# Other SBUF addresses for the weight parts and the activation parts of a two-layer hybrid decoder on one core

## The reference, cut to what matters

```
h = rmsnorm(x); proj = h @ w_in                    # 1024 -> 10752 columns
A = dilated attention of 3 head groups; B = retention with decay, 4 heads
m = sigmoid(ga) * (A @ w_a) + sigmoid(gb) * (B @ w_b)
x = x + m @ w_o
x = x + relu(rmsnorm(x) @ w_up)**2 @ w_down        # 1024 -> 4096 -> 1024
```

## The kernel before

| tensor | before | after |
|---|---|---|
| h_hi, h_lo | 32, 32 | 32, 112 |
| w_hi slot 0, slot 1 | 32, 32 | 0, 16 |
| w_lo slot 0, slot 1 | 32, 32 | 32, 40 |
| z_hi, z_lo (also u) | 0, 0 | 96, 64 |
| m_hi, m_lo | 0, 0 | 0, 32 |
| y_hi, y_lo | 0, 0 | 64, 96 |
| x, w_raw | 32, 32 | 0, 0 |
| tables, rstd_all, decay, mask | 32 | 64 |
| the float32 tensors of attention and retention | 0 | 0 |
| ssum, sq, hn, relu, relu2, diag, gdiag (and others that share the end of the zone) | 0 | 0 |

## Time and profile before

### The profile page before, as it was taken

One profiled execution on the slowest core, in us unless ns is written; L12 is line 12 of the kernel. 1 busy time (PEld: TensorE's weight loads), 2 busy tenths in 40 slices (PEclk: granted clock), 3 DMA queues, 4 the chain that ended last, 5 costly groups with the idle time before them and its releaser, 6 DMA issues.

```text
span 1973.8 us, 26960 instructions
## 1 busy us (share of the span) xinstructions
PE 1957.8 (99%) x9580; PEld 1619.1 (82%) x9580; DVE 1110.7 (56%) x1764; ACT 730.5 (37%) x1124; POOL 91.5 (5%) x71
## 2 busy tenths in 40 slices
PE   8999999999999999999999999999999999999999
PEld 7987878887888888888899878888778888888887
DVE  5466675847446635444635574847655575445355
ACT  5134535354223323223322535453532233223233
POOL 0010110200000000000001110201000000000000
PEclk9999999999999999999999999999999999999999
DMA  4432322323232323232333322323233333323332
GB/s 135 128 91 65 101 83 65 102 65 96 93 98 89 105 85 106 85 106 85 106 110 86 91 81 76 91 65 102 61 101 96 97 95 97 101 90 97 94 96 76
DMA packets 208845, 182.20 MB, mean 92 GB/s; under 512 B 12624, under 2 KB 197072, under 8 KB 208496
## 3 DMA queue, kind: packets, MB, share of 16 engines
q1 hardware_dynamic: 208464, 180.65, 30.0%
q10 hardware_dynamic: 288, 0.28, 0.0%
HBM read 178.68 MB, written 2.23 MB: 92 GB/s over the span
## 4 chain that ended last, share of the span: by engine, by line
PE 95%; DVE 1%; ACT 1%; issue 1%; DMA 1%; SPq 0%; DVEq 0%; ACTq 0%
PE pj L1180 26%; PE pj L1182 25%; PE pj L1181 25%; PE rb L1327 2%; PE pj L1367 2%; PE sc L1270 2%; PE yo L1296 2%; PE pj L1368 2%; PE pj L1369 2%; PE pt L1280 1%; PE sc L1230 1%; PE sc L1232 1%; PE pt L1230 1%; PE pt L1232 1%; PE sc L1231 1%; PE pt L1231 1%
## 5 line engine op out<-in xcount | busy, mean ns | idle before, releaser
L1180 PE MATMUL pj<-h_hi,w_hi 128*128 128x512 f32 x1408 | 557.1, 396 | 0.0
L1182 PE MATMUL pj<-h_hi,w_lo 128*128 128x512 f32 x1408 | 548.5, 390 | 0.0
L1181 PE MATMUL pj<-h_lo,w_hi 128*128 128x512 f32 x1408 | 548.5, 390 | 0.0
L464 ACT CAST w_hi<-w_raw 128x1024 fp32r<-128x1024 f32 x330 | 331.7, 1048 | 395.8 <-PE pj L1182 263.5
L748 DVE TENSOR_TENSOR w_lo<-w_raw,w_hi 128x1024 fp32r<-128x1024 f32 x330 | 398.5, 1248 | 118.1 <-ACT w_hi L464 117.2
L1180 PEld LDWEIGHTS pj<-h_hi,w_hi 128*128 128x128 f32 x1408 | 264.2, 188 | 62.5 <-issue 6.9
L1181 PEld LDWEIGHTS pj<-h_lo,w_hi 128*128 128x128 f32 x1408 | 264.4, 188 | 56.0 <-issue 2.4
L1182 PEld LDWEIGHTS pj<-h_hi,w_lo 128*128 128x128 f32 x1408 | 264.3, 188 | 55.8
L1180 PE MATMUL pj<-z_hi,w_hi 128*128 128x512 f32 x640 | 253.2, 396 | 0.0
L1181 PE MATMUL pj<-z_lo,w_hi 128*128 128x512 f32 x640 | 253.2, 396 | 0.0
L1182 PE MATMUL pj<-z_hi,w_lo 128*128 128x512 f32 x640 | 253.2, 396 | 0.0
(11 more groups left out here) (169 smaller groups left out, 2301.8 us busy)
## 6 DMA issues: line engine op xcount, KB each, us to landing
w_raw<-in_w_in SPq DMA_DIRECT2D x152, 512.0 KB, 4.2
w_raw<-in_w_up SPq DMA_DIRECT2D x64, 512.0 KB, 4.0
w_raw<-in_w_down SPq DMA_DIRECT2D x64, 512.0 KB, 3.8
w_raw<-in_w_b SPq DMA_DIRECT2D x16, 512.0 KB, 4.1
w_raw<-in_w_o SPq DMA_DIRECT2D x16, 512.0 KB, 4.1
spread_share<-row_scratch SPq DMA_DIRECT2D x16, 256.0 KB, 3.9
w_raw<-in_w_a SPq DMA_DIRECT2D x8, 512.0 KB, 3.5
x_nat<-in_x SPq DMA_DIRECT2D x2, 1024.0 KB, 6.5
```

The lines of the kernel that those rows point to most:

```text
L464: nc.scalar.copy(w_hi[s][:, c], raw[:, c]).then_inc(hi_done, 1)
L1180: nc.tensor.matmul(out, w_hi[s][:, wc], acts[0], start=first, stop=False)
L1181: nc.tensor.matmul(out, w_hi[s][:, wc], acts[1], start=False, stop=False)
L1182: return nc.tensor.matmul(out, w_lo[s][:, wc], acts[0], start=False, stop=last)
```

## The change

Only addresses change. No instruction, wait or transfer is added, removed or moved: on each engine the program stands in the same order, with the same operations on the same shapes. Small fillers are put ahead of x, h_hi and h_lo, three tensors (h_lo and the second slots of w_hi and w_lo) get 8 more columns and are used from 16, 16 and 8 bytes behind their start, and the tensors of the zone that z, m and y share are placed one by one. The two names of the gate scratch, sA and sB, and the scratch that begins at `pad` move by a few hundred bytes with them.

```diff
-        fill = -nc.sbuf_base % 512
-        if fill:
-            sb("fill", [P, fill // 4], F32)
+        def phase(name, to):
+            base = -(-nc.sbuf_base // 32) * 32
+            fill = (to - base) % 128
+            if fill:
+                sb(name, [P, fill // 4], F32)
+        def shifted(name, n, skip):
+            return sb(name, [P, n + 8], F32R)[:, skip // 4:skip // 4 + n]
+        phase("fill_x", 0)
         x = sb("x", [P, KT, S], F32)
+        phase("fill_h_hi", 32)
         h_hi = sb("h_hi", [P, KT, S], F32R)
-        h_lo = sb("h_lo", [P, KT, S], F32R)
+        phase("fill_h_lo", 96)
+        h_lo = shifted("h_lo", KT * S, 16).rearrange("p (k s) -> p k s", k=KT)
         raw = sb("w_raw", [P, 2048], F32)
-        w_hi = [sb(f"w_hi{i}", [P, 2048], F32R) for i in range(2)]
-        w_lo = [sb(f"w_lo{i}", [P, 2048], F32R) for i in range(2)]
+        w_hi = [sb("w_hi0", [P, 2048], F32R), shifted("w_hi1", 2048, 16)]
+        w_lo = [sb("w_lo0", [P, 2048], F32R), shifted("w_lo1", 2048, 8)]
...
-        zone0 = -(-nc.sbuf_base // 512) * 512
+        zone0 = -(-nc.sbuf_base // 128) * 128
...
-        m_hi = at("G", "m_hi", [P, KT, S], F32R)
-        m_lo = at("G", "m_lo", [P, KT, S], F32R)
-        z_hi = at("G", "z_hi", [P, KT, S], F32R)
-        z_lo = at("G", "z_lo", [P, KT, S], F32R)
-        pad = top["G"]
-        y_hi = at("G", "y_hi", [P, KA, S], F32R)
-        y_lo = at("G", "y_lo", [P, KA, S], F32R)
+        def at_phase(name, k, to):
+            base = top.get("G", zone0)
+            top["G"] = base + (to - base % 128 + zone0 % 128) % 128
+            return at("G", name, [P, k, S], F32R)
+        m_hi = at_phase("m_hi", KT, 0)
+        m_lo = at_phase("m_lo", KT, 32)
+        z_hi = at_phase("z_hi", KT, 96)
+        z_lo = at_phase("z_lo", KT, 64)
+        pad = top["G"] + 64
+        y_hi = at_phase("y_hi", KA, 64)
+        y_lo = at_phase("y_lo", KA, 96)
+        top["G"] += 32
         sB = at("G", "sB", [P, 2, S], F32)
-        top["G"] += 5120
+        top["G"] = zone0 + 89 * 1024
         sA = at("G", "sA", [P, 2, S], F32)
```

## The result

| | before | changed |
|---|---|---|
| median us | 1977.8 (4 runs, 1976.58 to 1978.74) | 1996.62 (4 runs, 1996.01 to 1998.19) |
| the profiled execution | 1975.57 | 1996.29 |
| its span | 1973.8 | 1994.5 |

The ratio is 1.0097, 95% interval 1.0079 to 1.0114: the changed kernel is 1% slower, by 19 us where 11 were forecast. The lines of the code moved by 18 behind the edit (L1180 to L1182 are now L1198 to L1200).

The account below looks back on a forecast made before the run. PE, busy in 99% of the span, was taken to bound the kernel by its distances between matmul starts. Terms 15.8 - 5.5 + 0.8 = +11.1 us gave 1988 us; forecast 1978 to 1998, full range 1950 to 2008.

Parts of the forecast that it names:

- (a): 4224 matmuls with h moving: from 226.7 to 231.1 ns, 4.4 ns more on 3600 of them, +15.8 us.
- (d): Starts 16 or 8 bytes off in h_lo and the second weight slots: taken as 0, 6 us at most.
- single distances seen by weight slot: PE's trace after: the two weight slots may show different distances, unit by unit, proving that single distances matter; no size given.
- (b): 2496 matmuls with z, m and y moving: from 233.3 to 231.1 ns, -5.5 us; bounds -16.5 and +16.7 us.
- (c): Value products: 192 of 576 with 512 columns go from 226.7 to 231.1 ns, +0.8 us; 768 of 256 columns stay.
- (e): ACT and DVE casts and subtractions on the moved tensors: any lengthening hidden behind PE, waits near 11 us; transfers 0.
- z rhythm everywhere: Rival: any distance but 0 costs 233.3 ns, so h loses 23.8 us; 2001 us, 2007 with (d); chance 0.15, or worse included.
- A modest gain: Rival: distance 0 isn't the best, staggered pairs run faster; 1945 or 1961 us, if h's mean stays below 229 ns; chance 0.19.
- No change: Rival: z's slowness comes from its upper SBUF place or from addresses above 128 bytes, not the distance; 1977 us; chance 0.11.
- All interference gone: Rival: staggering removes all the excess per matmul, 127 us in all; 1850 us; chance 0.09.

Follow-up runs that it names:

- the first kernel on the pair that meets: Kernel before, with h_hi, w_hi, m_hi, z_lo, y_hi at 32 and h_lo, w_lo, m_lo, z_hi, y_lo at 96 modulo 128: 1997.38 us.
- The first experiment: Kernel before, with z, m and y moved to 32 modulo 128 like h and the weights: 1977.64 us, ratio 1.0003.
- the third and fourth scans: Kernel before, weights at 32 (slot 0) and 48 (slot 1) modulo 256; h at 32, then 208, with m, z, y moved too: 1977.16, then 1987.39 us.

## Why the prediction was right, and where it was off

**The direction and the mechanism held.** The forecast was 1988, slower; measured is 1996.6. No wait changed by more than 0.5 us, no engine but PE by more than 2 us, and h left its 226.7 ns. Against the +11.1 us of the sum the two spans differ by 20.7: h is 7.3 above its term, z, m and y 3.1, all else 0.7, and the values are 1.5 below theirs.

That 231.1 ns fits h so well is in part luck. I took it from nine matmuls that had distance 0 and came behind a float32 matmul; no row tied it to mixed distances. Of the mixtures measured later some ran at 231.1, but h's in the first kernel on the pair that meets ran at 232.2. And mixing isn't what costs: the uniform distances of 192 and 224 cost more, 233.3.

**(a), h, was sized 15.8 us and measured 23.1.** Three things are in the difference. The rate out of rhythm, 231.1 ns, was right for h's mixture at multiples of 32: 231.0 without the small shifts. The count was low: I left out 630 matmuls behind the restarts, but over all 4156 the mixture costs 17.1 us, 4.1 ns each. And the rest is (d).

**(d), the starts off 32 bytes, was the term that I mis-sized.** I bounded it by 6 us and took 0. The two kernels with and without the shifts differ by 6.0 us on h. Their profiled spans differ by 2.5 us (1994.5 against 1992.0), since z, m and y ran 0.9 us shorter with the shifts than without, the values 0.6, and the small matmuls and distances over 300 ns 2.0; their medians differ by 3.7 (1996.6 against 1992.9). The sign that the prediction named, single distances seen by weight slot, came only in part: in the changed kernel h's units of slot 0 run at 233.1, but those of slot 1 at 231.3 and at 233.3, so something besides the addresses counts here too. The two kernels also differ in the distances themselves by 8 and 16, so this is the cost of the shifts here, not a price of misalignment by itself. That 16 bytes off can cost much more is shown by the kernel with all at 48, 28 us above all at 32.

**(b), z, m and y, was sized -5.5 us and measured -2.4.** Out of rhythm z was to come to 231.1; it came to 232.4. With the same z addresses it did run at 231.1 against weights at 32 (-4.3 us), but at 233.3 against weights at 0 and 32. So mixtures of distances don't share one rate, as I took them to, but run at one of several between 231 and 233.3.

**(c), the values.** 512 columns +0.7 us where +0.8 was taken; 256 columns -1.4 us where 0 was.

**(e)** held: casts of 1047 ns and subtractions of 1250, waits unchanged.

**The reading of the distance was wrong in its modulus.** I took it modulo 128 as the change does, and the table of distances ahead of the prediction has a 0 for h that is 128 modulo 256. Modulo 256 its h distances are 160, 144 (w_hi with h_hi), 240, 224 (w_hi with h_lo) and 128, 120 (w_lo with h_hi). The forecast did not hang on it, since by either modulus h becomes a mixture. The first experiment did, and it missed.

**The rivals.** *z rhythm everywhere* gave 2001 and has come nearest to what happened: h at 232.7, z at 232.4. *A modest gain* fell with h's mean at 232.7 where its rule asked for less than 229. *No change* fell: the same instructions take 1961.7, 1977.6, 1990.0 and 2001.4 us by addresses alone. But one of its two reasons was half right: something in the addresses above 128 bytes does count, since z at 0 modulo 128 and 128 modulo 256 from the weights stayed at 233.3. The two independent read ports of which the Trainium skill's page "TensorE: Matmul & The Clock Gate" speaks (section "Step-by-step: what each phase is for") don't keep the operands' addresses from counting here. *All interference gone* did not happen in any of the kernels; no even stream of 512 columns was below 226.7.

## What to carry to other kernels

Where TensorE is busy throughout and streams moving operands of 4 bytes at the high clock, read the distance from start to start in each long stretch, and compare stretches that differ only in what they read. If they differ, the addresses are a free thing to try: putting all the operands at one address modulo 256, a multiple of 32, gave 0.75% here, while staggering them cost 1%. The address tried for all was 32; h and the weights alone ran as well at 160. Don't settle a modulus or a "good" distance from one pair of stretches; change one tensor's address and look whether its own stretch moves, in every stage and layer, since one stretch can run at another rate than the next with the same addresses.

## What the runs showed of the hardware that I had not expected

- The rate of a stream of products of 512 float32r columns depends on addresses modulo 256: a distance of 0 gave 226.7 ns with both operands at 32 or 160, 32, 128, 176, 192 and 224 gave 233.3, 48 and 64 gave 233.1 and 229.4, but 160 and 240 gave 227.1 and 226.7 (h in the third and fourth scans). A distance of 256 (modulo 512) was as good as 0, and 128 was not. Each distance but 0, 192 and 224 comes from one kernel, and 48, 64, 160, 176 and 240 from units that alternate with another distance.
- The even streams lie mostly at few rates. Per triple of products they are 680 ns (226.7), 687 (229.1), 693 (231.1) and 700 (233.3): steps of about 6.7 ns, in which 16 columns pass at 2.4 GHz. Some streams lie between them, at 230.0 and at 232.2 to 232.7 ns.
- Addresses alone don't set the rate: with all at 48 it was 231.0 ns in the gates and 233.3 in the MLP of the first layer, and the reverse in the second layer of the same execution, and in the changed kernel the two slot-1 units of an h part ran at 231.3 and 233.3. What else sets it is open.
- Weight loads of 64 columns for 128 (134 ns for 188) came with a distance of 230.0 ns for 226.7. Why the excess is there, and which two reads meet, stays open; neither of the two pairings that I tried explains the rates.
